# Modulation sums of a decoder trunk: five of eight weight units moved from TensorE to GpSimd and VectorE, and one weight unit moved behind the gate units in the load order

## What is computed

```python
c_act = silu(c)                                  # (1, 1024)
for l in range(2):
    mod = c_act @ w_ada[l] + b_ada[l]            # (1, 6144), a 24 MB matrix
    shift1, scale1, gate1, shift2, scale2, gate2 = split(mod, 6)
    h = rmsnorm(x, norm1_g[l]) * (1 + scale1) + shift1
    u_b, u_c, u_h, u_q, u_k, u_v = split(h @ w_in[l])        # 1024 x 3072
    y_conv = u_b * conv3(u_c * u_h)
    y_att = attention(rope(rmsnorm(u_q)), rope(rmsnorm(u_k)), u_v)
    y_mix = concat(rmsnorm(y_conv), rmsnorm(y_att))
    x = x + gate1 * (y_mix @ w_out[l])                       # 1024 x 1024
    h2 = rmsnorm(x, norm2_g[l]) * (1 + scale2) + shift2
    x = x + gate2 * hier_moe(h2)     # 16 experts, each 1024 x 256 (twice) and 256 x 1024
```

## Time and profile before

| what | us |
|---|---|
| median of 3 runs (lowest to highest) | 573.7 (573.54 to 575.43) |
| the profiled execution's own time | 575.47 |
| its span | 573.7 |
| TensorE busy | 549.2 |
| VectorE busy | 278.2 |
| ScalarE busy | 224.1 |
| GpSimd busy | 17.0 |
| HBM traffic | 189.8 MB, 331 GB/s on average |

### The profile page before, as it was taken

One profiled execution on the slowest core, in us unless ns is written; L12 is line 12 of the kernel. 1 busy time (PEld: TensorE's weight loads), 2 busy tenths in 40 slices (PEclk: granted clock), 3 DMA queues, 4 the chain that ended last, 5 costly groups with the idle time before them and its releaser, 6 DMA issues.

```text
span 573.7 us, 8078 instructions
## 1 busy us (share of the span) xinstructions
PE 549.2 (96%) x3258; PEld 356.9 (62%) x3258; DVE 278.2 (49%) x475; ACT 224.1 (39%) x386; POOL 17.0 (3%) x74
## 2 busy tenths in 40 slices
PE   7899999999999999999979999999998999999996
PEld 6568959768675444443348896886786644444433
DVE  3629974993481122222377398489438202222233
ACT  2527545632356222221256355554224632222121
POOL 3105000000000000000000000000000000000000
PEclk9899999999999999999998999999999999999999
DMA  8999994972999999999999744498296389999971
GB/s 303 388 387 367 401 380 162 424 304 97 426 409 412 413 415 411 413 414 414 404 386 387 272 146 146 165 421 371 74 381 279 146 302 394 413 414 412 414 289 76
DMA packets 51759, 189.79 MB, mean 331 GB/s; under 512 B 4650, under 2 KB 4730, under 8 KB 44292
## 3 DMA queue, kind: packets, MB, share of 16 engines
q1 hardware_dynamic: 50496, 185.62, 82.7%
q0 software_dynamic: 896, 2.45, 1.3%
q10 hardware_dynamic: 324, 1.13, 0.6%
HBM read 188.12 MB, written 1.06 MB: 330 GB/s over the span
## 4 chain that ended last, share of the span: by engine, by line
PE 70%; DVE 17%; DMA 6%; ACT 3%; issue 2%; SPq 1%; DVEq 0%; ACTq 0%
PE ps L1574 18%; PE ps L1600 9%; PE ps L1471 7%; PE ps L1554 6%; PE ps L1363 6%; PE ps L1356 6%; PE ps L1251 5%; DVE wlo L793 5%; PE ps L1616 4%; DMA raw<-in_w_ada_dram 4%; DMA raw<-in_w_in_dram 2%; DVE work L955 2%; DVE cbc L1008 1%; PE ps L1306 1%; DVE tokmaj L950 1%
## 5 line engine op out<-in xcount | busy, mean ns | idle before, releaser
L793 DVE TENSOR_TENSOR wlo<-raw,whi 128x1024 fp32r<-128x1024 f32 x64 | 75.5, 1220 | 30.5 <-ACT whi L503 30.4
L503 ACT ACTIVATE whi<-raw 128x1024 fp32r<-128x1024 f32 x64 | 65.4, 1057 | 31.3 <-PE ps L1356 14.3
L1574 PE MATMUL ps<-raw,qkT 128*64 128x512 f32 x256 | 58.3, 597 | 1.6 <-ACT work L743 1.6
L1600 PE MATMUL ps<-raw,work 128*64 128x512 f32 x256 | 58.4, 598 | 0.0
L1574 PE MATMUL ps<-raw,cbc 128*64 128x512 f32 x256 | 57.5, 594 | 0.0
L1188 DVE SCALAR_TENSOR_TENSOR work<-ps,cw,work 128x256 f32<-128x256 f32 x16 | 10.9, 683 | 95.8 <-ACT work L737 95.8
L1356 PE MATMUL ps<-act_hi,whi 128*128 128x256 f32 x192 | 54.9, 286 | 0.0
L1174 DVE TENSOR_TENSOR v_sb<-ps,gates 128x512 f32<-128x512 f32 x32 | 22.0, 691 | 67.5 <-PE ps L1600 67.5
L1356 PE MATMUL ps<-act_hi,wlo 128*128 128x256 f32 x192 | 54.3, 283 | 0.0
L1356 PE MATMUL ps<-act_lo,whi 128*128 128x256 f32 x192 | 54.3, 283 | 0.0
L1251 PE MATMUL ps<-raw,c_rep 128*32 128x512 f32 x384 | 45.6, 606 | 2.9 <-DMA raw<-in_w_ada_dram 2.9
(11 more groups left out here) (241 smaller groups left out, 865.5 us busy)
## 6 DMA issues: line engine op xcount, KB each, us to landing
raw<-in_w_ada_dram SPq DMA_DIRECT2D x40, 1024.0 KB, 12.8
raw<-in_w_gate_dram SPq DMA_DIRECT2D x64, 512.0 KB, 9.3
raw<-in_w_up_dram SPq DMA_DIRECT2D x64, 512.0 KB, 11.2
raw<-in_w_down_dram SPq DMA_DIRECT2D x32, 1024.0 KB, 12.2
raw<-in_w_in_dram SPq DMA_DIRECT2D x23, 1024.0 KB, 14.6
raw<-in_w_ada_dram SPq DMA_DIRECT2D x16, 512.0 KB, 11.6
raw<-in_w_out_dram SPq DMA_DIRECT2D x8, 1024.0 KB, 6.3
gates<-gate_line POOLq DMA_DIRECT2D x2, 1024.0 KB, 5.0
```

The costliest lines, as they stand in the source:

```text
L503: act.activation(whi[:, slot(n), :], raw[:, r, (i % 2) * 1024:(i % 2 + 1) * 1024], ACT.Copy).then_inc(hi_done, 1)
L793: dve.tensor_tensor(wlo[:, slot(n), :], raw[:, ring_slot[("w", l, i // 2)], (i % 2) * 1024:(i % 2 + 1) * 1024], whi[:, slot(n), :].bitcast ...
L1574: ins = pe.matmul(ps[i * SLOTS:(i + 1) * SLOTS, 0, :], hg[p // 2 % 2][:, k, c0:c0 + SLOTS], ws[i][:, :, kk, :], start=(k == 0), stop=(k == ...
L1600: ins = pe.matmul(ps[i * SLOTS:(i + 1) * SLOTS, 2 + n, :], hidT[:, p % 2, kk, i * SLOTS:(i + 1) * SLOTS], ws[i][:, c0:c0 + 512], start=(kk ...
```

## The change

Three things change; the line numbers of the program shift by some 7 to 40.

1. In `stream`, unit w11 is loaded behind G0 to G7 instead of ahead of them.
2. Of the eight M units TensorE does 0 and 1 ahead of the sum of squares, and 2 behind `values`. GpSimd multiplies units 3, 4 and 5 by `c_act` and adds them into `acc` (which is `qkT`), VectorE adds units 6 and 7 to it with one instruction each, behind its last split of the layer. TensorE adds `acc` into bank 6 with a matrix of ones (`ada_pool_sum`), inside the output projection. `ada_out`, `ada_cols` and `modulation` of M stand later in their engines' lists. The slots of M3 to M7 are released by the new semaphore `acc_used`.
3. The transposes of the attention output come behind the second half of the output projection instead of the first.

```diff
+POOL_FROM = 3
+DVE_FROM = 6
...
+        pe_steps = [POOL_FROM + 1 if kind == "M" else n for (kind, _), n in zip(chunks, chunk_units)]
+        units_before = [sum(pe_steps[:i]) for i in range(len(chunks) + 1)]
+        pool_units = KD - POOL_FROM
+        acc = qkT[:, :, :, :].rearrange("p w c s -> p (w c s)")
...
-            stream += [("w", l, u) for u in range(3 if l == 0 else 2, 12)]
+            stream += [("w", l, u) for u in range(3 if l == 0 else 2, 11)]
             stream += [("a", chunk_of[("G", l)], k) for k in range(KD)]
-            stream += [("w", l, u) for u in range(12, 16)]
+            stream += [("w", l, u) for u in range(11, 16)]
...
+                if kind == "a" and chunks[l][0] == "M" and i >= POOL_FROM:
+                    sp.wait_ge(acc_used, pool_units * chunks[l][1] + i - POOL_FROM + 1)
...
         @block.gpsimd
...
+                pool.wait_ge(csum_done, l + 1)
+                for k in range(POOL_FROM, DVE_FROM):
+                    unit = ("a", chunk_of[("M", l)], k)
+                    r = ring_slot[unit]
+                    pool.wait_ge(raw_full[r], landed[unit])
+                    product = acc if k == POOL_FROM else raw[:, r, :]
+                    pool.tensor_scalar(product, raw[:, r, :], c_rep[:, k, 0:1], None, ALU.mult
+                                       ).then_inc(pool_prod, 1)
+                    pool.wait_ge(pool_prod, (DVE_FROM - POOL_FROM) * l + k - POOL_FROM + 1)
+                    if k == POOL_FROM:
+                        pool.sem_inc(acc_used, 1)
+                    else:
+                        if k > POOL_FROM + 1:
+                            pool.wait_ge(acc_used, pool_units * l + k - POOL_FROM)
+                        pool.tensor_tensor(acc, raw[:, r, :], acc, ALU.add).then_inc(acc_used, 1)
...
         @block.scalar
...
-                ada_out("M", l)
                 split_half(l, 30)
...
                 split_half(l, 31)
+                ada_out("M", l)
...
         @block.vector
...
                 split_half(l, 30)
-                modulation("M", l)
...
                 split_half(l, 31)
+                for k in range(DVE_FROM, KD):
+                    unit = ("a", chunk_of[("M", l)], k)
+                    dve.wait_ge(raw_full[ring_slot[unit]], landed[unit])
+                    dve.wait_ge(acc_used, pool_units * l + k - POOL_FROM)
+                    dve.scalar_tensor_tensor(out=acc, in0=raw[:, ring_slot[unit], :], scalar=c_rep[:, k, 0:1], in1=acc,
+                                             op0=ALU.mult, op1=ALU.add).then_inc(acc_used, 1)
...
                 dve.reciprocal(stat[:, 0:1], stat[:, 2:3]).then_inc(rstd_ready, 1)
+                modulation("M", l)
                 dve.wait_ge(unit_used, n0 + 32)
...
         @block.tensor
...
+            def ada_pool_sum(l):
+
+                pe.wait_ge(acc_used, pool_units * (l + 1))
+                for i in range(4):
+                    ins = pe.matmul(ps[32 * i:32 * i + 32, 6, :], ones[:, 0:32], acc[:, i * 512:(i + 1) * 512],
+                                    start=False, stop=True, skip_group_check=True)
+                ins.then_inc(ada_used, 1)
...
                 in_half(23, 4, 6, False)
+                ada_acc("M", l, range(0, 2))
                 pe.wait_ge(csq_ready, l + 1)
...
                 values(1)
-                ada_acc("M", l, range(0, 8))
+                ada_acc("M", l, range(2, POOL_FROM))
...
-                    if half == 0:
-                        ada_cols("M", l)
+                    if half == 1:
                         pe.wait_ge(yatt_ready, l + 1)
...
                 ins.then_inc(row_done, 1)
+                ada_pool_sum(l)
                 for half in range(4):
                     ins = out_half(1, half, 1, (0,))
                 ins.then_inc(row_done, 1)
+                ada_cols("M", l)
                 for half in range(4):
                     out_half(1, half, 1, (1,)).then_inc(unit_used, 1)
```

More of the change, by code:

```diff
@@ L176, in trunk @@
         ada_used = sem("ada_used")
+        acc_used = sem("acc_used")
+        pool_prod = sem("pool_prod")
         mod_evac = sem("mod_evac")
@@ L271, in trunk @@
         chunk_units = [4 if kind in ("A0", "A1") else KD for kind, _ in chunks]
-        units_before = [sum(chunk_units[:i]) for i in range(len(chunks) + 1)]
+        pe_steps = [POOL_FROM + 1 if kind == "M" else n for (kind, _), n in zip(chunks, chunk_units)]
+        units_before = [sum(pe_steps[:i]) for i in range(len(chunks) + 1)]
+        pool_units = KD - POOL_FROM
+        acc = qkT[:, :, :, :].rearrange("p w c s -> p (w c s)")
         def in_unit(u):
@@ L360, in wait_free @@
                 kind, l, i = unit
-                if kind == "a":
+                if kind == "a" and chunks[l][0] == "M" and i >= POOL_FROM:
+                    sp.wait_ge(acc_used, pool_units * chunks[l][1] + i - POOL_FROM + 1)
+                elif kind == "a":
                     sp.wait_ge(ada_used, units_before[l] + i + 1)
@@ L1252, in ada_acc @@
                                         raw[:, ring_slot[unit], i * 512:(i + 1) * 512],
-                                        start=(k == 0), stop=(k == chunk_units[q] - 1), skip_group_check=True)
+                                        start=(k == 0), stop=(kind != "M" and k == chunk_units[q] - 1),
+                                        skip_group_check=True)
                     ins.then_inc(ada_used, 1)
+            def ada_pool_sum(l):
[4 more added lines that the diff above has]
+                ins.then_inc(ada_used, 1)
             def first_cols(a):
```

## The result

The changed kernel takes 597.3 us (595.2 to 598.2, 4 runs) against 574.1 for the one before in the same comparison: a ratio of 1.039, 95% interval 1.037 to 1.042. The forecast was 564.9, the range ended at 590. The profiled execution took 595.16 us with a span of 593.4. The sign that the forecast gave 0.59 was wrong; what happened is the rival in which GpSimd and VectorE shut each other out, dearer than priced there (587.1, with 592 as its upper end).

The account below looks back on a forecast made before the run. Bound: DMA stream from 140.7 us to layer 0's end, elsewhere TensorE and VectorE in turn. Gains of 4.7 us in layer 0 and 4.1 in layer 1 gave 573.7 - 8.8 = 564.9 us; range 562 to 590.

Parts of the forecast that it names:

- The sign that the forecast gave 0.59: Whole kernel: faster by over 0.3%, against 0.05 for within 0.3% and 0.36 for slower.
- the rival in which GpSimd and VectorE shut each other out: Ahead of the projection, their instructions alternate; 11.1 us lost in each layer, 587.1 us; chance 0.33 (580 to 592).
- Where the time goes (what bounds the kernel): TensorE and VectorE alternate ahead of 140 us and in layer 1; DMA stream bounds layer 0 from 140.7 us.
- one rival: End of layer 0: TensorE sets the last expert pair, or load rate falls; half of 4.7 lost, 567.2 us; chance 0.04.
- Term 1, w11: Loads of w11 behind G: TensorE's wait for G7 goes, gaining 1.1 us in layer 0 and 0.5 in layer 1.
- Terms 2, 3, 4 and 6: Around the projection: start 4.5 us earlier, 3.6 left after the closing sum, A1 3.6 earlier, VectorE's two units hidden.
- Term 5, GpSimd hidden: Behind the sum of squares: GpSimd's products and additions take 13.5 us, end at 131.6 (127.8 to 141.2), hidden before 137.1.

Follow-up runs that it names:

- the best kernel: The changed kernel without GpSimd's work: TensorE does units 0 to 3, VectorE units 4 to 7; 564.2 us, ratio 0.9825 to the kernel before.
- w11 alone: The kernel before with only the load of w11 moved behind G0 to G7; 571.3 us, ratio 0.994.
- the products alone: The kernel before with w11 behind G, plus three unused GpSimd products per layer and no additions; 579.6 us, ratio 1.010.

## Why the prediction was wrong

- **Where the time goes (what bounds the kernel).** Right for the stretch ahead of the projection in both layers. For the load stream in layer 0 it holds for the kernel before; in the best kernel the chain of layer 0 no longer closes through the load of w0 but through TensorE's last expert pair, as one rival had it. Its residual addition stands at 288.8 instead of 294.1. Of these 5.3 us 1.6 are there at 36 us already (the same matmul starts at 34.80 and 36.37), ahead of everything that the change touches, so layer 0 gained about 3.7 against the forecast 4.7.
- **Term 1, w11.** Right in sign; 3 us against 1.6. In the changed kernel TensorE waited 0.3 us for G7 and not 1.1. Where the other half came from I did not isolate. Part of the difference between the two profiled executions cannot be the change: 0.6 us of it is there at 36 us, and the first load that moved is issued at 49 us.
- **Terms 2, 3, 4 and 6.** Right in sum, where GpSimd is absent, which shows them together and not one by one: 564.2 measured against 564.9, with VectorE's four units in the place of GpSimd's three and VectorE's two. The two kernels differ by 7.1 us from w11 alone (571.3), and the terms gave 7.2. A unit on VectorE took 2.35 us (2.3 forecast), the closing sum 1.0 (0.9). The projection began 7.4 us behind the sum of squares' end (7.5).
- **Term 5, GpSimd hidden.** This is the step that failed, in two ways. Its cost to others was put at nothing, on the ground that "no row shows that". The absence of a row was no evidence, and the cost is the whole loss: 16.6 us of VectorE's time per layer, of which the 2 us that the forecast had between heads ready (129.0) and needed (131.0) cover a little. Given back, that share brings the time from 597.3 to 567.7. Its own cost was taken from copies, 1.93 us a product; it is 5.4, above even the upper bound of 4.6, and GpSimd ends at 142.6, behind the latest forecast (141.2). The closing sum did not wait for it, since VectorE's own part came later still (149.5 instead of 137.1). The additions, put at 3.9, take 4.5, as the Trainium skill has it (GPSIMD Engine Reference, 3.1).
- **The rival.** It had the mechanism (VectorE's instructions stand behind GpSimd's one by one) and gave 587.1, 10 us too little. It put 11.1 us of waiting, all ahead of the split convolution; 4.7 fall there, and 11.9 on L1055, L817 and L1063 behind it, which the transposes need. Less the 2 us of slack that makes 14.6 per layer, 7 us more in both. The rest is the clock, which neither it nor the forecast had: transposes at 1.97 us instead of 0.93 twice, and 48 matmuls at 11.4 and 12.1 us instead of 10.9, together 3.8. The two add up to 10.8 where 10.2 are missing.
- **The chances.** The Trainium skill (SBUF — State Buffer, "Who interferes with whom") stated the rule outright. Nothing in the trace spoke against it; 0.33 for it was too little.

## What to carry to other kernels

Before work is moved to GpSimd, list what VectorE does in the same microseconds: an instruction with two operands in SBUF, and a single-operand TENSOR_SCALAR like L1063 too (the reciprocals here were not), can stand still for nearly as long as GpSimd's lasts. Here long GpSimd instructions ran beside a chain of short VectorE ones on the critical path, and cost 4%; in the expert stage, where VectorE is a fifth busy, no cost showed. VectorE's own waits were the better home here: 2.35 us a unit, and 1.8% faster than before. Where the trace has no row for a pairing of engines, its cost is unknown and not nothing; one run with the work added and unused prices it.

## What the runs showed of the hardware

- A GpSimd product over 2048 elements takes 5.44 us, over 1024 2.77 to 2.85, with a constant or a scalar from a tile alike; an addition 4.54 and 2.18; a copy of 1024 1.04.
- An addition of 2048 holds VectorE until about 0.1 us before its recorded end (4.60 us for an instruction of 0.69 that began 0.5 us behind its start); a product of 2048 lets it go 1.9 us before. An instruction that begins 0.4 us into a product is held too (L1048 at 121.65; 3.88 us at 127.45 beside the products alone). One that followed another without a gap as a product began got through (L1055 at 132.02, 0.68), and the product then took 6.41 us instead of 5.44. Why that one passed is not shown.
- Not held in any row looked at: an instruction with one SBUF tensor and one PSUM operand (0.69 us, begun 0.5 us into a product of 1024), and a reciprocal with one SBUF operand (1.75 us, begun 0.5 us into a product and 0.7 into an addition of 2048). For the PSUM operand there is no row that begins within an addition.
- TensorE's granted clock was 0.50, the lower level, behind waits of 5.8 and 7.5 us, and 0.51 some 3 us behind one of 2.1; its matmuls then take about twice as long (12 in 5.46 us instead of 2.95).
